# Output products of four branches in a two-layer trunk: one fp32 product, or three fp32r passes over high and low parts

## The chip, the cores and the metric

One core of a Trainium2 chip runs the whole program. The metric is the device time of one execution in microseconds; the time before is the median of three runs, 2294.9 us (2294.73 to 2297.84).

## The reference

Two layers of a hybrid decoder trunk on 512 tokens of width 1024. Per layer:

```
h = rms_norm(x, mix_norm_g[l])
p_gdn, p_mla, p_rwkv, p_dsa, p_gate = _split(h @ w_in[l], SLAB_SPLITS)
y_a = gdn_mixer(p_gdn, ...) @ w_out_gdn[l]
y_b = mla_mixer(p_mla, ...) @ w_out_mla[l]
y_c = rwkv7_mixer(p_rwkv, ...) @ w_out_rwkv[l]
y_d = dsa_mixer(p_dsa, ...) @ w_out_dsa[l]
g_a, g_b, g_c, g_d = _split(sigmoid(p_gate), GATE_SPLITS)
merged = g_a * y_a + g_b * y_b + g_c * y_c + g_d * y_d
x = x + merged @ w_o[l]
hm = rms_norm(x, mlp_norm_g[l])
x = x + square(relu(hm @ w_up[l])) @ w_down[l]
```

Each mixer's output is 512 tokens by 256 features, each `w_out_*` is 256 by 1024, each gate matrix 1024 by 1024. All is float32.

## The kernel before

Everything is held feature-major: a tile is 128 features by 512 tokens. Weights come as a stream of 134 units per layer (`unit_list`, L56), each a block of 1024 by 128 (8 tiles of 128x128), in the order of use. SyncE loads unit g into `ring[g % 3]` (L393). The large products are made in three passes over high and low parts, both of type fp32r: ScalarE copies the unit, rounded, to `w_hi[g % 2]` (`split_next`, L1046), GpSimd subtracts in two instructions of 128x512 to get `w_lo` (L425), and `split_product` (L458) multiplies `w_hi` by `h_hi` and `h_lo` (L464, L465, 16 matmuls), then waits for `split_lo` and multiplies `w_lo` by `h_hi` (L468, 8 matmuls). ScalarE calls `split_next` once for each unit whose product it has taken from its bank, and it has called it twice ahead of the first: after it has taken unit g it splits unit g + 2, so that two units at most are in split form. GpSimd follows it in the order of units.

The part of interest is the merge. Per branch there are eight "merge" units, the gate columns of 128 output features each, and with each comes an output block, 256 by 128 of that branch's `w_out`, which SyncE loads to `out_ring[n % 6]` (L398); n counts merge units over the whole program, 64 in all. TensorE makes the gates two at a time (`gates`, L500: two times 24 matmuls, into banks that ScalarE reads), and then the two outputs (`merge_outputs`, L518): each is two fp32 matmuls of 128x128 by 128x512 from `out_ring` and `yo` (L525). The branch output stands in `yo[:, slot]`, two buffers of 2x512 columns, written by VectorE (L1643 for RWKV, L1710 for DeltaNet, L1478 piece by piece in the two attentions). ScalarE takes a gate from its bank with a sigmoid into `sg[n % 2]` (`merge_sig`, L1009), before that waiting until output n - 2 has been merged (`mg_done`), and calls `split_next`. VectorE multiplies the output's bank by the gate and adds it to `mg` (`merge`, L1433), and signals `mg_done`.

Where the merges stand: RWKV (branch 2) has four outputs in one group (L784 to L788) and two pairs; DeltaNet (branch 0) four pairs, spread over the index scores of the sparse attention (L851 to L858); sparse attention (branch 3) a group of four after its own attention (L867 to L870) and two pairs; MLA (branch 1) a group of four (L917 to L920) and two pairs. In the groups of four of branches 3 and 1 the first two gates were made piecewise inside the attention (`gate_pieces`, L528). So a layer has 3 groups of four and 10 pairs. All engines run their queues strictly in the order of the code, each on its own, tied by semaphores.

GpSimd's queue holds, beside the subtractions, a few DMAs that wait: L435 (rotary tables) behind unit ("ds", 0), L438 behind unit ("merge", 3, 2).

Of the kernel before, what the change touches and what calls it, by code (L numbers as in the profile page):

```python
# [22 lines left out]
P = 128  # L23
# [134 lines left out]
def build(nc, x_in, pos_in, wstream, par_in, const_in, tabs, x_dram, out):  # L158
    ctx = ExitStack()
    with ctx:  # L160
# [11 lines left out]
        out_ring = sb("out_ring", [P, OUT_RING, 2, P])  # L172
# [4 lines left out]
        yo = sb("yo", [P, 2, 2, T])  # L177
# [74 lines left out]
        for name, n in (  # L252
# [20 lines left out]
            ("m_ss", 16), ("m_p", 16), ("m_pn", 16), ("m_pt", 16), ("m_o", 16),  # L273
            ("mg_sig", 32), ("mg_raw", 4), ("mg_done", 32), ("mg_hi", 8), ("mg_lo", 8), ("wo_done", 8), ("up_relu", 32), ("up_sq", 32), ("up_hi", 32), ("up_done", 32), ("g_zs", 1), ("r_s0", 1), ("g_s0", 1), ("down_done", 8 * QUARTERS),
# [49 lines left out]
        def merges_to(g):  # L324
# [32 lines left out]
            v=ar(25, (TT, 256)), tab=ar(27, (2, T)), ikz=ar(29, (2, T)), kz=ar(31, (2, 2, T)), tmp=ar(35, (T,)),  # L357
# [3 lines left out]
            tab=ar(17, (2, T)), tmp=ar(19, (T,)), bias=ar(20, (T,)), kr=ar(21, (T,)),  # L361
# [83 lines left out]
        def _(pe):  # L445
# [65 lines left out]
            def merge(l, br, slot, i, output=None):  # L511

                numbers = gates(l, br, i)
                if output:
                    pe.wait_ge(S[output], at(l, output, per[output]))
                merge_outputs(slot, numbers)
# [203 lines left out]
            for l in range(L):  # L720
# [65 lines left out]
                pe.wait_ge(S["r_out"], at(l, "r_out", 1))  # L786
                merge_outputs(0, numbers)
                merge_outputs(0, more)  # L788
# [15 lines left out]
                merge(l, 2, 0, 2)  # L804
                merge(l, 2, 0, 3)
# [36 lines left out]
                pe.wait_ge(S["d_vf"], at(l, "d_vf", 2))  # L842
                for half in range(2):
# [7 lines left out]
                for qt in range(1, TT):  # L851
                    if qt > 1:
                        index_scores(qt)
                    merge(l, 0, 1, qt - 1)
# [3 lines left out]
                merge(l, 0, 1, 3)  # L858
# [9 lines left out]
                pe.wait_ge(S["d_o"], at(l, "d_o", 16))  # L868
                merge_outputs(0, numbers)
                merge_outputs(0, more)  # L870
# [9 lines left out]
                merge(l, 3, 0, 2)  # L880
# [27 lines left out]
                merge(l, 3, 0, 3)  # L908
# [9 lines left out]
                pe.wait_ge(S["m_o"], at(l, "m_o", 16))  # L918
                merge_outputs(1, numbers)
                merge_outputs(1, more)  # L920
                for i in range(2, 4):
                    merge(l, 1, 1, i)
# [36 lines left out]
        def _(act):  # L959
# [48 lines left out]

            def merge_sig(l):  # L1009
                for _ in range(2):  # L1010
# [7 lines left out]
                    split_next()  # L1018

            def piecewise_sig(l, i):  # L1020

                if i in (GATE_STEPS[5], GATE_STEPS[11]):
# [5 lines left out]
                    split_next()  # L1028

# [54 lines left out]
            for l in range(L):  # L1084
# [88 lines left out]
                merge_sig(l)  # L1173
                merge_sig(l)
# [36 lines left out]
                for i in range(8):  # L1211
                    if i == 7:
# [29 lines left out]
                attention(l, "d", Dv, lambda i: piecewise_sig(l, i))  # L1242
                late_sig(l)
# [19 lines left out]
                attention(l, "m", Mv, lambda i: piecewise_sig(l, i))  # L1263
                late_sig(l)
# [43 lines left out]
        def _(dve):  # L1308
# [141 lines left out]
            def attention(l, x, V, scale, bias, slot, fill):  # L1450
# [517 lines left out]
```

## Time and profile before

| what | value |
|---|---|
| median of 3 runs | 2294.9 us |
| the profiled execution, its own time | 2294.88 us |
| its span | 2293.1 us |
| granted TensorE clock, mean over the span | 0.964 |
| TensorE matmuls busy | 2129.2 us, 93% |
| VectorE busy | 1241.2 us, 54% |
| ScalarE busy | 720.8 us, 31% |
| GpSimd busy | 740.5 us, 32% |

The profile is of one execution. The chain that ended last is followed back from the last instruction to the first, at each step to what released it. A row of the timeline merges instructions of one kind that follow each other on an engine; what stands in brackets is the engine's idle time before them and who ended it. fp32 matmuls appear as two instructions each. Ends of matmuls are modelled, with the next one's start ahead of them: the pace is read from starts.

### The profile page before, as it was taken

Reading aid. Unit: us, or ns where it says so; the run is one execution under the profiler, and the core shown is the slowest. Engines: PE = TensorE matmul, PEld = TensorE weight load, DVE = VectorE, ACT = ScalarE, POOL = GpSimd, SP = SyncE. Lnnn points to the kernel's source line nnn. Section 1 sums busy time; section 2 is a strip of 40 time slices with the busy share of each in tenths; the row PEclk is TensorE's granted clock in tenths of the full one; section 3 lists DMA queues with packets and bytes.
Section 4 is the critical chain, followed back from the end, with each engine's and each line's share of the span. In section 5 each row is a group of like instructions: output and inputs, shape, how many; then the busy total and the mean of one; then the engine's idle time right before and its main releaser. Section 6 shows DMA issues by size and latency. Waiting matters only on the chain.

```text
span 2293.1 us, 34619 instructions
## 1 busy us (share of the span) xinstructions
PE 2129.2 (93%) x14488; PEld 1654.4 (72%) x14488; DVE 1241.2 (54%) x1930; ACT 720.8 (31%) x1100; POOL 740.5 (32%) x550
## 2 busy tenths in 40 slices
PE   5988898998999999999989888899989999999997
PEld 3777677766666788888868766777656668888886
DVE  6785765798654332222358766568966544222223
ACT  3421321332333342323243133123242433423322
POOL 1530321332212444444434012123222144444442
PEclk7999998998999999999989999989999999999998
DMA  4320200221121232332232001012212122332321
GB/s 158 103 71 3 67 29 30 78 81 57 45 94 51 83 117 93 95 98 92 92 103 92 26 28 59 30 46 77 67 48 92 44 78 92 95 99 92 101 93 65
DMA packets 52266, 170.03 MB, mean 74 GB/s; under 512 B 5648, under 2 KB 13968, under 8 KB 51600
## 3 DMA queue, kind: packets, MB, share of 16 engines
q1 hardware_dynamic: 50928, 162.75, 22.2%
q0 software_dynamic: 1184, 5.07, 0.6%
q8 instruction: 116, 1.90, 0.3%
q14 instruction: 38, 0.31, 0.0%
HBM read 160.45 MB, written 7.34 MB: 73 GB/s over the span
## 4 chain that ended last, share of the span: by engine, by line
PE 76%; DVE 20%; ACT 2%; issue 2%; DMA 1%; SPq 0%; DVEq 0%; ACTq 0%
PE bank_a L464 11%; PE bank_a L465 11%; PE bank_a L468 11%; PE bank_v L468 7%; PE bank_v L464 7%; PE bank_v L465 6%; PE bank_v L583 5%; PE bank_v L525 3%; DVE arena L1752 2%; DVE m L1750 2%; DVE arena L1325 2%; PE bank_v L699 2%; DVE s_z L1425 1%; PE bank_v L681 1%; DVE mg L1331 1%
## 5 line engine op out<-in xcount | busy, mean ns | idle before, releaser
L425 POOL TENSOR_TENSOR w_lo<-ring,w_hi 128x512 fp32r<-128x512 f32 x536 | 734.1, 1392 | 1383.1 <-ACT w_hi L1046 1383.0
L464 PE MATMUL bank_a<-h_hi,w_hi 128*128 128x512 f32 x1440 | 587.3, 408 | 7.8 <-DVE h_lo L1359 4.8
L465 PE MATMUL bank_a<-h_lo,w_hi 128*128 128x512 f32 x1440 | 566.3, 393 | 0.0
L468 PE MATMUL bank_a<-h_hi,w_lo 128*128 128x512 f32 x1440 | 356.5, 390 | 0.0
L1046 ACT ACTIVATE w_hi<-ring 128x1024 fp32r<-128x1024 f32 x268 | 281.7, 1051 | 234.9 <-DVE arena L1867 220.5
L464 PEld LDWEIGHTS bank_a<-h_hi,w_hi 128*128 128x128 f32 x1440 | 272.9, 190 | 88.7 <-issue 18.8
L465 PEld LDWEIGHTS bank_a<-h_lo,w_hi 128*128 128x128 f32 x1440 | 273.6, 190 | 63.9 <-issue 9.3
L468 PEld LDWEIGHTS bank_a<-h_hi,w_lo 128*128 128x128 f32 x1440 | 270.8, 188 | 57.1 <-POOL w_lo L425 0.6
L1325 DVE TENSOR_TENSOR sg<-bank_v,sg 128x512 f32<-128x512 f32 x112 | 77.5, 692 | 339.7 <-PE bank_v L468 256.9
L464 PE MATMUL bank_v<-parts,w_hi 128*128 128x512 f32 x640 | 254.4, 398 | 1.4 <-DVE parts L1838 1.4
L465 PE MATMUL bank_v<-parts,w_hi 128*128 128x512 f32 x640 | 253.4, 396 | 0.0
L1857 DVE TENSOR_TENSOR arena<-arena 128x512 f32<-128x512 f32 x64 | 44.3, 692 | 244.8 <-ACT arena L1289 244.7
L468 PE MATMUL bank_v<-parts,w_lo 128*128 128x512 f32 x640 | 162.2, 396 | 0.0
L464 PEld LDWEIGHTS bank_v<-parts,w_hi 128*128 128x128 f32 x640 | 120.3, 188 | 32.7 <-DVE parts L1838 4.1
L465 PEld LDWEIGHTS bank_v<-parts,w_hi 128*128 128x128 f32 x640 | 120.2, 188 | 29.5 <-issue 0.5
L468 PEld LDWEIGHTS bank_v<-parts,w_lo 128*128 128x128 f32 x640 | 120.2, 188 | 29.1
L583 PE MATMUL bank_v<-arena 64*64 64x64 f32 x3712 | 114.1, 221 | 4.2 <-DVE arena L1397 4.2
L583 PEld LDWEIGHTS bank_v<-arena 64*64 64x64 f32 x3712 | 113.2, 138 | 4.9 <-DVE arena L1397 4.7
L525 PE MATMUL bank_v<-yo,out_ring 128*128 128x512 f32 x256 | 114.0, 592 | 0.0
L1325 DVE TENSOR_TENSOR arena<-arena 128x512 f32<-128x512 f32 (+5 forms) x80 | 96.7, 1209 | 23.4 <-ACT arena L1102 20.8
L1289 ACT ACTIVATE arena<-bank_a 128x512 f32<-128x512 f32 x64 | 38.3, 598 | 205.3 <-PE bank_a L468 205.3
L1016 ACT ACTIVATE sg<-bank_a 128x512 f32<-128x512 f32 x56 | 33.4, 597 | 217.8 <-PE bank_a L468 108.4
(277 smaller groups left out, 2450.3 us busy)
## 6 DMA issues: line engine op xcount, KB each, us to landing
ring<-in_w SPq DMA_DIRECT2D x268, 512.0 KB, 3.5
out_ring<-in_w SPq DMA_DIRECT2D x64, 128.0 KB, 3.5
x_dram<-arena SPq DMA_DIRECT2D x2, 2048.0 KB, 7.6
arena<-x_dram SPq DMA_DIRECT2D x2, 2048.0 KB, 7.9
arena<-in_x SPq DMA_DIRECT2D x2, 1024.0 KB, 8.7
arena<-tabs POOLq DMA_DIRECT2D x4, 512.0 KB, 3.9
out_x<-arena SPq DMA_DIRECT2D x2, 1024.0 KB, 4.3
par<-in_par POOLq DMA_DIRECT2D x2, 937.0 KB, 7.2
```

Source lines behind the costliest of these rows:

```text
L425: ins = nc.gpsimd.tensor_tensor(w_lo[:, g % SPLIT, ks, :], raw, w_hi[:, g % SPLIT, ks, :].bitcast(F32), ALU.subtract)
L464: mm(b[:], w_hi[:, s, k, :], hi[:, k, :], start=k == 0, stop=False)
L465: mm(b[:], w_hi[:, s, k, :], lo[:, k, :], start=False, stop=False)
L468: ins = mm(b[:], w_lo[:, s, k, :], hi[:, k, :], start=False, stop=k == KT - 1)
L525: ins = mm(b[:], out_ring[:, n % OUT_RING, k, :], yo[:, slot, k, :], start=k == 0, stop=k == 1)
L583: ins = mm(b[quarter(p_), k * C:(k + 1) * C], lhs[quarter(p_), m, :], rhs(m, p_), start=True, stop=True)
L699: ins = mm(b[rows, 0:P], v[:, k, h * C:(h + 1) * C], V_pt(x)[:, j % 2, k, :], start=k == 0, stop=k == qt)
L1046: act_fn(w_hi[:, g % SPLIT, :, :], ring[:, g % RING, :, :], ACT.Copy).then_inc(S["split_hi"], 1)
L1325: link(v.tensor_tensor(out_, a, b, op))
L1750: link(v.max(m8[:], src))
L1752: link(v.match_replace(wk, m8[:], src, -3e38))
L1857: v.tensor_tensor(relu2[:, n % 2, :], relu[:, n % 2, :], relu[:, n % 2, :], MUL).then_inc(S["up_sq"], 1)
```

## The change

The 64 outputs are made from high and low parts in three fp32r passes. ScalarE makes `out_hi` (one copy of 128x256 for each output block, `split_out`, right behind `split_next` of the same gate), GpSimd makes `out_lo` in place over `out_ring`. It does so for the output block of unit g - 2 behind its subtraction of unit g. TensorE waits for `ow_lo` at each output and makes six matmuls in place of two. The branch output stands in the arena, and ScalarE copies it to `y_hi` (2 x 128x512), VectorE subtracts to `y_lo` (2 x 128x512), once per branch and layer; there is one pair of such buffers, so that `y_hi` of a branch waits until the branch before is merged. The DMA of the rotary tables moves behind unit ("ds", 1).

```
-        out_ring = sb("out_ring", [P, OUT_RING, 2, P])
+        out_hi = sb("out_hi", [P, OUT_RING, 2, P], F32R)
+        with nc.sbuf_tensor("out_ring", [P, OUT_RING, 2, P], F32) as out_ring:
+            pass
+        out_lo = sb("out_lo", [P, OUT_RING, 2, P], F32R)
-        yo = sb("yo", [P, 2, 2, T])
+        y_hi = sb("y_hi", [P, 2, T], F32R)
+        y_lo = sb("y_lo", [P, 2, T], F32R)
...
                 ins.then_inc(S["split_lo"], 1)
+                if g >= SPLIT and UNITS[(g - SPLIT) % NU][0] == "merge":
+                    n = merges_to(g - SPLIT)
+                    pool.wait_ge(S["ow_hi"], n + 1)
+                    slot = n % OUT_RING
+                    nc.gpsimd.tensor_tensor(out_lo[:, slot, :, :], out_ring[:, slot, :, :], out_hi[:, slot, :, :].bitcast(F32), ALU.subtract).then_inc(S["ow_lo"], 1)
...
-                if UNITS[u] == ("ds", 0):
+                if UNITS[u] == ("ds", 1):
...
-            def merge_outputs(slot, numbers):
-                for j in range(2):
+            def merge_outputs(numbers):
+                for n in numbers:
                     b, reader, emptied = banks.next("v", "mg_done")
                     pe.wait_ge(reader, emptied)
-                    n = numbers[j]
-                    pe.wait_ge(out_here[n % OUT_RING], 16 * (n // OUT_RING + 1))
+                    pe.wait_ge(S["ow_lo"], n + 1)
+                    hi, lo = out_hi[:, n % OUT_RING], out_lo[:, n % OUT_RING]
                     for k in range(2):
-                        ins = mm(b[:], out_ring[:, n % OUT_RING, k, :], yo[:, slot, k, :], start=k == 0, stop=k == 1)
+                        mm(b[:], hi[:, k, :], y_hi[:, k, :], start=k == 0, stop=False)
+                        mm(b[:], hi[:, k, :], y_lo[:, k, :], start=False, stop=False)
+                    for k in range(2):
+                        ins = mm(b[:], lo[:, k, :], y_hi[:, k, :], start=False, stop=k == 1)
                     ins.then_inc(v_full, 1)
...
+            def split_out(n):
+
+                slot = n % OUT_RING
+                act.wait_ge(out_here[slot], 16 * (n // OUT_RING + 1))
+                act_fn(out_hi[:, slot, :, :], out_ring[:, slot, :, :], ACT.Copy).then_inc(S["ow_hi"], 1)
+
+            def high_output(l, src, need, k, branch):
+
+                act.wait_ge(S[need], at(l, need, k))
+                act.wait_ge(S["mg_done"], at(l, "mg_done", 8 * branch))
+                for f in range(2):
+                    act_fn(y_hi[:, f, :], src[:, f, :], ACT.Copy).then_inc(S["y_hi"], 1)
...
                     act_fn(sg[:, n % 2, :], b[:], ACT.Sigmoid).then_inc(S["mg_sig"], 1)
                     sigs[0] += 1
                     split_next()
+                    split_out(n)
...
+            def low_output(l, src, branch):
+
+                for f in range(2):
+                    dve.wait_ge(S["y_hi"], at(l, "y_hi", 2 * branch + f + 1))
+                    v.tensor_tensor(y_lo[:, f, :], src[:, f, :], y_hi[:, f, :].bitcast(F32), SUB).then_inc(S["y_lo"], 1)
```

`high_output` and `low_output` stand: for RWKV behind the first two gates of the group of four (ScalarE) and behind the last product of its output (VectorE); for DeltaNet at the fifth "ds" unit; for the two attentions at their ends. `piecewise_sig` calls `split_out` as `merge_sig` does. TensorE waits for `y_lo` where it waited for the branch output. SyncE's queue is as before.

How the queues move, at two places. First GpSimd around the last merge units of branch 2 (`w_lo` is a weight unit's low part, `out_lo` an output block's). Before:

```order
L425 TENSOR_TENSOR w_lo<-ring,w_hi 128x512 [waits split_hi]
L425 TENSOR_TENSOR w_lo<-ring,w_hi 128x512
L435 DMA arena<-tabs 128x2x512 [waits r_u,tab_out]
L425 TENSOR_TENSOR w_lo<-ring,w_hi 128x512 [waits split_hi]
L425 TENSOR_TENSOR w_lo<-ring,w_hi 128x512
```

And of the change, the same place with one unit more:

```order
L430 TENSOR_TENSOR w_lo<-ring,w_hi 128x512 [waits split_hi]
L430 TENSOR_TENSOR w_lo<-ring,w_hi 128x512
L436 TENSOR_TENSOR out_lo<-out_ring,out_hi 128x256 [waits ow_hi]
L430 TENSOR_TENSOR w_lo<-ring,w_hi 128x512 [waits split_hi]
L430 TENSOR_TENSOR w_lo<-ring,w_hi 128x512
L436 TENSOR_TENSOR out_lo<-out_ring,out_hi 128x256 [waits ow_hi]
L445 DMA arena<-tabs 128x2x512 [waits r_u,tab_out]
L430 TENSOR_TENSOR w_lo<-ring,w_hi 128x512 [waits split_hi]
```

Each subtraction of an output block stands behind both subtractions of the weight unit that is two further on.

Second TensorE at the last pair of branch 2 (`bank_a` takes a gate, `bank_v` an output; the second wait of an output is for its bank's last reader). Before:

```order
L468 MATMUL bank_a0<-h_hi,w_lo 128x512 [waits split_lo]
L468 MATMUL bank_a0<-h_hi,w_lo 128x512 x7
L525 MATMUL bank_v1<-yo,out_ring 128x512 [waits out_here0,g_row]
L525 MATMUL bank_v1<-yo,out_ring 128x512
L525 MATMUL bank_v2<-yo,out_ring 128x512 [waits out_here1,g_row]
L525 MATMUL bank_v2<-yo,out_ring 128x512
L558 MATMUL bank_a1<-consts,arena 128x128 [waits mg_sig,g_prep]
```

Of the change:

```order
L478 MATMUL bank_a0<-h_hi,w_lo 128x512 x7
L532 MATMUL bank_v1<-y_hi,out_hi 128x512 [waits ow_lo,g_row]
L533 MATMUL bank_v1<-y_lo,out_hi 128x512
L532 MATMUL bank_v1<-y_hi,out_hi 128x512
L533 MATMUL bank_v1<-y_lo,out_hi 128x512
L535 MATMUL bank_v1<-y_hi,out_lo 128x512 x2
L532 MATMUL bank_v2<-y_hi,out_hi 128x512 [waits ow_lo,g_row]
L533 MATMUL bank_v2<-y_lo,out_hi 128x512
L532 MATMUL bank_v2<-y_hi,out_hi 128x512
L533 MATMUL bank_v2<-y_lo,out_hi 128x512
L535 MATMUL bank_v2<-y_hi,out_lo 128x512 x2
L568 MATMUL bank_a1<-consts,arena 128x128 [waits mg_sig,g_prep]
```

The outputs' wait for a DMA has become a wait for GpSimd; nothing stands between the last gate and the two outputs, as before.

## Rows read from the trace of the kernel before

**Rows 1.** The page, the chain that ended last, shares of the span by engine.
```profile
PE 76%; DVE 20%; ACT 2%; issue 2%; DMA 1%; SPq 0%; DVEq 0%; ACTq 0%
```

**Rows 2.** The page, costliest groups: count, busy us, mean ns, idle before and releaser.
```profile
L525 PE MATMUL bank_v<-yo,out_ring 128*128 128x512 f32 x256 | 114.0, 592 | 0.0
```

**Rows 3.** Timeline, all engines, 597 to 613 us: start us, us, engine, line, operation.
```profile
597.87 1.98 PE L468 MATMUL bank_a<-h_hi,w_lo 128*128 128x512 f32 x8
...
603.31 1.98 PE L468 MATMUL bank_a<-h_hi,w_lo 128*128 128x512 f32 x8
605.12 7.03 PE L525 MATMUL bank_v<-yo,out_ring 128*128 128x512 f32 x16
...
608.61 0.60 ACT L1016 ACTIVATE sg<-bank_a 128x512 f32<-128x512 f32 x1 [13.17 <-DVE mg L1446]
...
610.23 2.95 POOL L425 TENSOR_TENSOR w_lo<-ring,w_hi 128x512 fp32r<-128x512 f32 x2 [12.07 <-ACT w_hi L1046]
```

**Rows 4.** Timeline, all engines, a pair of branch 0, 525 to 529 us.
```profile
525.15 3.59 PE L525 MATMUL bank_v<-yo,out_ring 128*128 128x512 f32 x8
525.35 0.60 ACT L1016 ACTIVATE sg<-bank_a 128x512 f32<-128x512 f32 x1 [3.89 <-PE bank_a L468]
525.84 1.05 ACT L1046 ACTIVATE w_hi<-ring 128x1024 fp32r<-128x1024 f32 x1
526.97 2.52 POOL L425 TENSOR_TENSOR w_lo<-ring,w_hi 128x512 fp32r<-128x512 f32 x2 [2.89 <-ACT w_hi L1046]
```

**Rows 5.** Groups by line and form, ScalarE: a form of 128x256.
```profile
L1209 ACT ACTIVATE arena<-bank_a 128x256 f32<-128x256 f32 x16 | 5.9, 383 | 5.3 <-DVE arena L1743 2.7 <-DVE arena L1740 2.0
```

**Rows 6.** Timeline, all engines, the group of four of branch 2, 267 to 278 us.
```profile
267.57 0.60 ACT L1016 ACTIVATE sg<-bank_a 128x512 f32<-128x512 f32 x1 [11.89 <-DVE mg L1442]
...
271.93 0.69 DVE L1442 TENSOR_TENSOR mg<-bank_v,sg 128x512 f32<-128x512 f32 x1 [1.02 <-PE bank_v L525]
...
278.02 7.87 PE L797 MATMUL bank_a<-consts,arena 128*128 128x128 f32 x48 [6.18 <-DVE arena L1660]
```

**Rows 7.** Timeline, all engines, a pair of branch 2, 299 to 310 us.
```profile
299.00 3.59 PE L525 MATMUL bank_v<-yo,out_ring 128*128 128x512 f32 x8
...
301.46 7.93 DVE L1325 TENSOR_TENSOR arena<-arena 128x1024 f32<-128x1024 f32 x4
301.56 8.98 POOL L425 TENSOR_TENSOR w_lo<-ring,w_hi 128x512 fp32r<-128x512 f32 x4 [27.44 <-ACT w_hi L1046]
```

**Rows 8.** Busy time by engine in windows, among the index scores: PE, PEld, DVE, ACT, POOL, PEclk.
```profile
434.00:552.00 118.00, 109.37 (x418) 77.40 (x416) 110.26 (x219) 36.20 (x56) 36.05 (x27) 0.97 0.22 69
```

**Rows 9.** Timeline, VectorE and ScalarE, first and last pair of branch 0.
```profile
474.88 0.69 DVE L1325 TENSOR_TENSOR sg<-bank_v,sg 128x512 f32<-128x512 f32 x1
...
546.90 0.60 ACT L1016 ACTIVATE sg<-bank_a 128x512 f32<-128x512 f32 x1 [20.01 <-DVE mg L1446]
...
551.10 0.92 DVE L1446 TENSOR_TENSOR mg<-mg,sg 128x512 f32<-128x512 f32 x1
```

**Rows 10.** Timeline, all engines, later pairs and the last group of four.
```profile
625.47 3.59 PE L525 MATMUL bank_v<-yo,out_ring 128*128 128x512 f32 x8
...
626.14 5.85 POOL L425 TENSOR_TENSOR w_lo<-ring,w_hi 128x512 fp32r<-128x512 f32 x4 [10.02 <-ACT w_hi L1046]
...
714.55 7.03 PE L525 MATMUL bank_v<-yo,out_ring 128*128 128x512 f32 x16
...
719.69 0.63 ACT L1272 ACTIVATE parts<-mg 128x512 fp32r<-128x512 f32 x1 [1.09 <-DVE mg L1446]
...
749.00 2.98 POOL L425 TENSOR_TENSOR w_lo<-ring,w_hi 128x512 fp32r<-128x512 f32 x2 [2.90 <-ACT w_hi L1046]
```

**Rows 11.** Timeline, TensorE, an idle wait in an attention.
```profile
663.99 0.30 PE L689 MATMUL bank_a<-consts,arena 128*128 128x128 f32 x1 [1.97 <-DVE arena L1471]
```

**Rows 12.** Windows behind waits of TensorE; columns as in rows 8.
```profile
665.10:668.40 3.30, 3.30 (x11) 2.27 (x10) 1.12 (x5) 0.66 (x3) 0.00 (x0) 0.50 0.01 3
...
276.00:282.70 6.70, 4.68 (x22) 4.68 (x23) 2.96 (x5) 2.50 (x4) 0.00 (x0) 0.50 0.11 45
```

More of the change, by code:

```diff
@@ L509, in gates, with merge @@
                 return numbers
[L511 to L516, printed above, removed]
-            def merge_outputs(slot, numbers):
-                for j in range(2):
+            def merge(l, br, i):
+                merge_outputs(gates(l, br, i))
+            def merge_outputs(numbers):
+                for n in numbers:
                     b, reader, emptied = banks.next("v", "mg_done")
                     pe.wait_ge(reader, emptied)
-                    n = numbers[j]
-                    pe.wait_ge(out_here[n % OUT_RING], 16 * (n // OUT_RING + 1))
+                    pe.wait_ge(S["ow_lo"], n + 1)
+                    hi, lo = out_hi[:, n % OUT_RING], out_lo[:, n % OUT_RING]
                     for k in range(2):
-                        ins = mm(b[:], out_ring[:, n % OUT_RING, k, :], yo[:, slot, k, :], start=k == 0, stop=k == 1)
+                        mm(b[:], hi[:, k, :], y_hi[:, k, :], start=k == 0, stop=False)
+                        mm(b[:], hi[:, k, :], y_lo[:, k, :], start=False, stop=False)
+                    for k in range(2):
+                        ins = mm(b[:], lo[:, k, :], y_hi[:, k, :], start=False, stop=k == 1)
                     ins.then_inc(v_full, 1)
@@ L785, in _ @@
                 more = gates(l, 2, 1)
-                pe.wait_ge(S["r_out"], at(l, "r_out", 1))
-                merge_outputs(0, numbers)
-                merge_outputs(0, more)
+                pe.wait_ge(S["y_lo"], at(l, "y_lo", 2))
+                merge_outputs(numbers)
+                merge_outputs(more)
                 pe.wait_ge(S["g_g"], at(l, "g_g", 2))
@@ L803, in _ @@
                     chunk_products("v", "g_row", half, G["g_of"], lambda m, p_: cst("upto")[quarter(p_), quarter(p_)])
-                merge(l, 2, 0, 2)
-                merge(l, 2, 0, 3)
+                merge(l, 2, 2)
+                merge(l, 2, 3)
                 pe.wait_ge(S["g_prep"], at(l, "g_prep", 1))
@@ L853, in _ @@
                         index_scores(qt)
-                    merge(l, 0, 1, qt - 1)
+                    merge(l, 0, qt - 1)
                     if qt == 2:
@@ L857, in _ @@
                             feat_group(("cq", i), l, h_hi, h_lo, "a", "m_in")
-                merge(l, 0, 1, 3)
+                merge(l, 0, 3)
                 numbers = []
@@ L867, in _ @@
                 more = gates(l, 3, 1)
-                pe.wait_ge(S["d_o"], at(l, "d_o", 16))
-                merge_outputs(0, numbers)
-                merge_outputs(0, more)
+                pe.wait_ge(S["y_lo"], at(l, "y_lo", 6))
+                merge_outputs(numbers)
+                merge_outputs(more)
                 pe.wait_ge(S["m_sq"], at(l, "m_sq", 1))
@@ L879, in _ @@
                 mm(b[:], cst("ones"), Mv["sq"][:, 2, :], start=True, stop=True).then_inc(v_full, 1)
-                merge(l, 3, 0, 2)
+                merge(l, 3, 2)
                 pe.wait_ge(S["m_c"], at(l, "m_c", 1))
@@ L917, in _ @@
                 more = gates(l, 1, 1)
-                pe.wait_ge(S["m_o"], at(l, "m_o", 16))
-                merge_outputs(1, numbers)
-                merge_outputs(1, more)
+                pe.wait_ge(S["y_lo"], at(l, "y_lo", 8))
+                merge_outputs(numbers)
+                merge_outputs(more)
                 for i in range(2, 4):
-                    merge(l, 1, 1, i)
+                    merge(l, 1, i)
                 for i in range(8):
```

32 lines of the change are left out of this document (22 added, 10 removed).

## Prediction, made before the changed kernel was run

> **What bounds the kernel now.** I read the chain that ended last first: TensorE holds 76% of the span and VectorE 20% [rows 1]. So what lengthens TensorE's own queue counts nearly everywhere, and what it must wait for counts too. The groups give the size of what is changed: the output products are 256 instructions and 114.0 us busy [rows 2]. GpSimd looks free in the shares, but each of its steps follows a ScalarE step, which follows a gate; the timeline around a merge shows this chain [rows 4], and there the change is decided.
>
> **What the new products save.** Two low passes of 8 matmuls in successive gates start 5.44 us apart, with 24 fp32r matmuls between [rows 3]: 0.227 us each. The group of four outputs takes 7.03 us for 16 fp32 instructions, the last of them 0.59 long, so (7.03 - 0.59) / 15 = 0.429 each [rows 2, 3]. An output falls from 4 x 0.429 = 1.72 us to 6 x 0.227 = 1.36 us. For 64 outputs that is 23 us, all of it on TensorE. This is the whole gain.
>
> **What the split costs by itself.** ScalarE's new copy of an output block has 256 columns. The nearest row of that width takes 0.38 us, a conversion of 512 columns 0.63 [rows 5, 10]: I take 0.42. GpSimd's new subtraction has 256 columns. Two of 512 take 2.52 us undisturbed [rows 4], so one takes 1.26; half of it is 0.63, the whole is the upper end, and I take 0.75, near the half. The copies and subtractions of the branch outputs (2 x 0.63 on ScalarE, 2 x 0.7 on VectorE, eight times) fall where both wait: ScalarE idles 11.89 us before the third sigmoid of a group and 20.01 before a late pair [rows 6, 9]. If that cover were gone they would cost 8 x 2 = 16 us; I take 3 us for all of this with the two extra copies in each attention.
>
> **The new wait.** The order of GpSimd's queue puts the low part of output n behind both subtractions of the weight unit two further on, and that unit is split by ScalarE only after it has taken gate n. For the first output of a pair this has happened a gate (5.44 us) earlier. For the second it has not even begun when TensorE arrives. Take the undisturbed pair [rows 4]. The outputs begin at 525.15, ScalarE takes the second gate at 525.35 and splits until 526.89, GpSimd works from 526.97 to 529.49. Only then comes the new subtraction, to 530.25, and TensorE can begin the second output at 530.3 and end it at 531.7. Now it is through at 525.15 + 8 x 0.429 = 528.6. So a pair loses 3.1 us, its own saving of 0.7 already counted. Behind TensorE's wait stand the next two gates, whose weights are long ready, so nothing fills it.
>
> Per layer there are ten pairs and three groups of four; the times of layer 0 follow.
>
> - Group of branch 2. The third sigmoid starts at 267.57 [rows 6], because it waits for the first output's merge. Split to 269.2, GpSimd to 271.8, new subtraction to 272.6, third output; then GpSimd's next unit to 275.1, 275.9, fourth output to 277.3, merged at 278.2 in place of 272.6 [rows 6]. TensorE's work at 278.02 waited for VectorE by then, so it moves too: +5.6.
> - Next pair. GpSimd needs 8.98 us for four subtractions here while VectorE works on two SBUF operands [rows 7]: 2.25 each, 1.8 times the quiet one. First half to 306.1, new subtraction (1.2) to 307.3, second half to 311.8, then 0.75 and 1.36: 314.0 instead of 299.00 + 3.44 = 302.4. +11.6.
> - Last pair of branch 2, quiet: +3.1.
> - The four pairs of branch 0 stand in a stretch where VectorE is busy 110.26 of 118 us and TensorE has slack [rows 8]. The first pair is taken at once by VectorE (its second output at 474.88 [rows 9]): +3.5. The next two are consumed tens of us later: 0. In the last one, ScalarE waits for VectorE until 546.90 [rows 9]; by the same steps, with TensorE at half its rate as it is there, the fourth merge ends at 559.3 instead of 552.0: +7.
> - Group of branch 3 [rows 3]. The third sigmoid moves from 608.61 to 608.25, split to 609.8, GpSimd 2.95 to 612.8, 613.6; its next unit to 616.4, 617.1; output to 618.5. Now 605.12 + 6.87 = 612.0: +6.5.
> - Its pairs. In the first, four subtractions run in one piece of 5.85 from 626.14 [rows 10]; with two new ones between, the second output ends at 635.0 against 625.47 + 3.44 = 628.9: +6.1. The second, with 2.98 for two subtractions as in a later pair [rows 10]: +3.6.
> - Group of branch 1: two copies of 0.63 into the merge's high part stand ahead of the third sigmoid [rows 10], so the sigmoid comes at 719.9, and the end at 730.0 against 714.55 + 6.87 = 721.4 [rows 10]: +8.6. Its pairs, with 2.98: +3.6 each, 7.2.
>
> Sum per layer: 5.6 + 11.6 + 3.1 + 3.5 + 7 + 6.5 + 6.1 + 3.6 + 8.6 + 7.2 = 62.8 us; the second layer repeats it: 126 us.
>
> **The clock.** TensorE now idles 4 to 8 us at each of these places. After an idle wait of 1.97 us in an attention [rows 11] it ran at 0.50 of full speed (1.2 GHz) from 665.1 to 668.4, with no idle time in it [rows 12]: 1.7 us lost. After 6.2 us of idle time the clock was 0.50 from 276.0 to 282.7 [rows 6, 12]. Outside branch 0 and the first group, where TensorE waits anyway, eight places per layer get such a wait on the path: 16 x 1.7 = 27 us if each is punished; bounds 0 and, at twice the price, 54. I take 22.
>
> A rule speaks of GpSimd's price beside VectorE. The row shows 2.25 us for what takes 1.26 alone [rows 7]. The Trainium skill, "SBUF — State Buffer", section "SBUF: two separate sides", says that the two share a port pair that is locked for a whole instruction, so that the loser blocks entirely. By it the new subtraction would be late by a whole VectorE instruction and not by a factor: 0.75 + 1.0 instead of 1.2 at the pair of branch 2, and likewise in the six places where 2.95 or more was needed for two; the sum would be some 12 us more. No row has a GpSimd instruction this short, so the trace does not decide it.
>
> Sum: the profiled execution, 2294.88 (span 2293.1), which is the median 2294.9 within 0.1 us; + 126 + 22 + 3 = **2446 us**, 6.6% slower. This kernel's measurement can tell about 0.2% (5 us) from no change.
>
> **Rivals.**
> - The wait is absorbed: part of it lies where TensorE or ScalarE later waits for VectorE, and the clock does not fall. For it: VectorE carries 20% of the chain. Against it: most places are followed by gates that run back to back. Half of the 126 and no clock loss: 2294.9 + 63 + 3 = 2361; two thirds, 2382.
> - Faster: TensorE never waits for `ow_lo`. Then only the products count: 2294.9 - 23 + 3 = 2275. The place is the second output of each pair; it decides if the low part is there 1.36 us after the outputs begin, at 526.5 in the pair of rows 4. Against it: GpSimd starts the subtraction ahead of it only at 526.97. It would need the queue order to be other than listed, or a change that does not do what it says.
> - Worse: the low clock persists between waits that lie 11 us apart, and the new subtraction costs nearly a full one. 54 for the clock, and 0.5 us for each of some 32 subtractions on the path, 16: 2295 + 126 + 54 + 16 + 3 = 2494.
>
> **The numbers.** Forecast: 0.72, of which a quarter for the port rule's 2458. Absorbed: 0.15. Worse: 0.10. Faster: 0.02, no change 0.01. The forecast's own bounds are 2420 (no clock loss, 0.63 us for each of the 32 subtractions on the path) and 2478 (54 us of clock loss). The range goes some 20 us further down, into the absorbed case, and a few up into the worse one: 2398 to 2482, which leaves out about 2 in 10. Faster by over 0.2%: 0.02; within: 0.01; slower: 0.97.
>
> **What would show it.** In the changed profile: an output of six matmuls in 1.36 us; TensorE idle ahead of the second output's first matmul (L532), 3 to 4 us in a pair, ended by GpSimd's L436, in all some 130 us; each L436 between 0.6 and 1.3 us long; GpSimd's share of the chain up from nothing to several per cent; a granted clock under the 0.964 of before; the MLP stretch unchanged. I am wrong if L532's idle time is below 60 us, if L436 comes before the unit's subtractions, or if the idle time is there and VectorE's waits shrink by as much.

## Result: 6.1% slower, and the profile after

The changed kernel takes 2435.8 us (median of four runs, 2429.0 to 2438.9); the kernel before took 2295.4 beside it (2294.7 to 2297.8). The ratio is 1.0608, with a 95% interval of 1.0585 to 1.0632. The profiled execution took 2438.2 us, with a span of 2436.4 and a mean granted clock of 0.939; before it was 2293.1 and 0.964. So the span grew by 143.3 us. The forecast was 2446.

The page of the changed kernel: the busy line, then the first line of the chain that ended last, to be set against [rows 1].

```profile
PE 2157.6 (89%) x14616; PEld 1706.3 (70%) x14616; DVE 1254.0 (51%) x1946; ACT 749.5 (31%) x1180; POOL 780.2 (32%) x614
...
PE 74%; DVE 15%; POOL 5%; ACT 3%; issue 2%; DMA 1%; SPq 0%; DVEq 0%; ACTq 0%
```

GpSimd stood in no part of the chain before and now holds 5% of it, though its busy share is 32% as before. This is a wait and not a load. TensorE, whose work was to shrink, is busy 28 us more, because many of its matmuls took longer each (the means below).

Groups by line; after the bar busy us, mean ns, idle before and its releaser. The first three answer to [rows 2].

```profile
L532 PE MATMUL bank_v<-y_hi,out_hi 128*128 128x512 f32 x128 | 67.3, 525 | 137.4 <-POOL out_lo L436 137.4
L533 PE MATMUL bank_v<-y_lo,out_hi 128*128 128x512 f32 x128 | 63.0, 492 | 0.0
L535 PE MATMUL bank_v<-y_hi,out_lo 128*128 128x512 f32 x128 | 52.9, 504 | 0.0
L436 POOL TENSOR_TENSOR out_lo<-out_ring,out_hi 128x256 fp32r<-128x256 f32 x64 | 54.4, 850 | 0.0
L1024 ACT ACTIVATE out_hi<-out_ring 128x256 fp32r<-128x256 f32 x64 | 26.1, 408 | 0.0
L1485 DVE TENSOR_TENSOR y_lo<-arena,y_hi 128x512 fp32r<-128x512 f32 x16 | 18.5, 1194 | 4.7 <-ACT y_hi L1031 4.6
```

One number explains most of the result: TensorE sat idle for 137.4 us ahead of L532, each time until GpSimd's L436. The means of 492 to 525 ns, against the 390 of a matmul at full clock, say that many of these products ran at the low clock (0.63 us each in the stretch at 1.2 GHz shown below).

The third pair of branch 0, the one that the prediction took as its model [rows 4], in the timeline of the changed kernel (start us, us, engine, line; in brackets the idle time before and who ended it).

```profile
560.14 0.40 PE L532 MATMUL bank_v<-y_hi,out_hi 128*128 128x512 f32 x1
...
560.34 0.60 ACT L1040 ACTIVATE sg<-bank_a 128x512 f32<-128x512 f32 x1 [3.59 <-PE bank_a L478]
...
560.83 1.05 ACT L1072 ACTIVATE w_hi<-ring 128x1024 fp32r<-128x1024 f32 x1
...
561.78 0.41 ACT L1024 ACTIVATE out_hi<-out_ring 128x256 fp32r<-128x256 f32 x1
561.96 2.49 POOL L430 TENSOR_TENSOR w_lo<-ring,w_hi 128x512 fp32r<-128x512 f32 x2 [2.19 <-ACT w_hi L1072]
...
564.41 0.73 POOL L436 TENSOR_TENSOR out_lo<-out_ring,out_hi 128x256 fp32r<-128x256 f32 x1
...
565.28 0.47 PE L532 MATMUL bank_v<-y_hi,out_hi 128*128 128x512 f32 x1 [3.58 <-POOL out_lo L436]
...
567.41 0.63 PE L474 MATMUL bank_a<-h_hi,w_hi 128*128 128x512 f32 x1
```

Read it from the sigmoid down. ScalarE takes the second gate at 560.34 and splits unit g + 2; GpSimd begins at 561.96 and needs 2.49 us for that unit, which TensorE does not want yet; only then come the 0.73 us that TensorE waits for. The second output starts 5.14 us after the first and not 1.39. The gates then resume at 567.41, 7.27 after the pair's start, where they took 3.03 before.

The clock behind this wait: busy time in a window (PE, PEld, DVE, ACT, POOL, then PEclk), as in [rows 12].

```profile
566.20:569.30 3.10, 3.10 (x9) 2.42 (x8) 2.96 (x8) 0.00 (x0) 0.00 (x0) 0.50 0.32 128
```

TensorE had been idle 3.58 us, had nothing to wait for from 565.28 on, and ran at 1.2 GHz from 566.2 to 569.3, so some 1.5 us are lost here.

The first pair behind the group of branch 2 answers to [rows 7].

```profile
308.00 7.30 DVE L1356 TENSOR_TENSOR arena<-arena 128x1024 f32<-128x1024 f32 x4
308.10 4.45 POOL L430 TENSOR_TENSOR w_lo<-ring,w_hi 128x512 fp32r<-128x512 f32 x2 [31.78 <-ACT w_hi L1072]
...
312.51 1.70 POOL L436 TENSOR_TENSOR out_lo<-out_ring,out_hi 128x256 fp32r<-128x256 f32 x1
...
314.18 4.46 POOL L430 TENSOR_TENSOR w_lo<-ring,w_hi 128x512 fp32r<-128x512 f32 x2
...
314.36 0.77 PE L532 MATMUL bank_v<-y_hi,out_hi 128*128 128x512 f32 x1 [8.65 <-POOL out_lo L436]
```

Here even the first output waits, 8.65 us. ScalarE comes late: it takes the pair's first gate only at 306.48, 0.8 us after TensorE has reached the outputs, so GpSimd begins only at 308.10. And GpSimd is slower beside VectorE, while both work on SBUF operands: its pair of subtractions takes 4.45 us in place of 2.49, and the new one 1.70 in place of 0.73.

### The profile page after: what moved, and what is told of

It reads as the page before. It is cut to its first block, busy times and chain, and to the rows that moved or that the text cites. A ratio compares the mean times of both kernels' runs of the same rounds, so it can differ in the third digit from the quotient of the medians.

```text
span 2436.4 us, 35047 instructions
## 1 busy us (share of the span) xinstructions
PE 2157.6 (89%) x14616; PEld 1706.3 (70%) x14616; DVE 1254.0 (51%) x1946; ACT 749.5 (31%) x1180; POOL 780.2 (32%) x614
## 4 chain that ended last, share of the span: by engine, by line
PE 74%; DVE 15%; POOL 5%; ACT 3%; issue 2%; DMA 1%; SPq 0%; DVEq 0%; ACTq 0%
PE bank_a L474 11%; PE bank_a L475 11%; PE bank_a L478 11%; PE bank_v L474 6%; PE bank_v L475 6%; PE bank_v L478 6%; PE bank_v L593 5%; POOL w_lo L430 4%; PE bank_v L709 2%; DVE s_z L1456 1%; ACT w_hi L1072 1%; POOL out_lo L436 1%; DVE arena L1356 1%; PE bank_v L691 1%; DVE mg L1362 1%
## 5 line engine op out<-in xcount | busy, mean ns | idle before, releaser
L430 POOL TENSOR_TENSOR w_lo<-ring,w_hi 128x512 fp32r<-128x512 f32 x536 | 722.5, 1369 | 1483.8 <-ACT w_hi L1072 1483.7
L532 PE MATMUL bank_v<-y_hi,out_hi 128*128 128x512 f32 x128 | 67.3, 525 | 137.4 <-POOL out_lo L436 137.4
L532 PEld LDWEIGHTS bank_v<-y_hi,out_hi 128*128 128x128 f32 x128 | 29.8, 233 | 162.7 <-issue 155.8
```

The costliest lines, as they stand in the source:

```text
L430: ins = nc.gpsimd.tensor_tensor(w_lo[:, g % SPLIT, ks, :], raw, w_hi[:, g % SPLIT, ks, :].bitcast(F32), ALU.subtract)
L532: mm(b[:], hi[:, k, :], y_hi[:, k, :], start=k == 0, stop=False)
```

## Experiments

Two questions were open. Is the loss the place of the split in GpSimd's and ScalarE's queues, and not the three passes? And why does the saving on TensorE not show? A first set of four kernels took the order, the passes and the clock apart (e1 to e4); of a second set, e5 to e7 priced the passes and the parts of the split work in the better order and e8 the clock once more; the last two split only half of the outputs. The expectation of each was written before it ran. The comparison kernel is always the kernel before, run on the same chip.

### e1_early: the output block is split with its own gate unit

```
-                if g >= SPLIT and UNITS[(g - SPLIT) % NU][0] == "merge":
-                    n = merges_to(g - SPLIT)
+                if UNITS[u][0] == "merge":
+                    n = merges_to(g)
```
```
     # at the end of split_next, in place of the two calls behind it
+                    if UNITS[g % NU][0] == "merge":
+                        split_out(merges_to(g))
```

> Every output block is split together with its own gate unit (ScalarE and GpSimd, two units ahead of the gate's product) and not two units later. Same work, same instructions, other order. Theory A (the loss is TensorE's wait for the late low part, and the clock that falls with it): the waits vanish, what is left is the saving of the products, 2295 - 23 + 3 to 8 for the splits = 2275 to 2290. Theory B (the loss is the added work on ScalarE, GpSimd and VectorE, and their contention): the order matters little, above 2380.

Measured: 2299.3 us, ratio 1.0016 (1.0008 to 1.0025). All 64 outputs are still split and made in three passes; only the place of two instructions in two queues differs, and 136.5 of the 140.4 us are gone. TensorE is not idle once ahead of L532 now. Its longest waits are others (waited for, us in total, times, longest):

```profile
PE bank_v L648 <- DVE s_z L1456: 29.1, 28, 1.3
PE bank_a L699 <- DVE arena L1508: 14.2, 9, 2.8
```

So the queue order is the cause of the loss. But the expected 2275 to 2290 was missed by 9 us: without that wait the kernel should have been 20 us faster than before and it is 4 slower. e5 to e7 follow that up.

### e2_pool_first: only GpSimd's order changed

The block with `out_lo` is moved ahead of the wait for `split_hi` of the next unit and of that unit's two subtractions. ScalarE still makes `out_hi` only behind the gate.

```
+                if g >= SPLIT and UNITS[(g - SPLIT) % NU][0] == "merge":
+                    ...
+                    nc.gpsimd.tensor_tensor(out_lo[:, slot, :, :], ...)
                 pool.wait_ge(S["split_hi"], g + 1)
```

> Only GpSimd's order changes: the subtraction of an output block goes ahead of the two subtractions of the weight unit two further on, ScalarE's order stays. Theory A: the second output of a pair waits for sigmoid, split, copy and one short subtraction, about 1.7 us in place of 3.6, and the pair loses 1.0 in place of 3.1; groups of four lose some 2.5 us less each. Per layer about 33 us of loss in place of 63, and less of the clock: 2360 to 2390. Theory B: as the change, 2425 to 2440.

Measured: 2362.8 us, ratio 1.0296 (1.0282 to 1.0310), inside Theory A's range. The third pair of branch 0 now waits 1.44 us and not 3.58. What stays is ScalarE's half of the chain, sigmoid, 1.05 us of `w_hi`, 0.41 of `out_hi`, then 0.72 on GpSimd:

```profile
PE bank_v L532 <- POOL out_lo L430: 85.8, 38, 9.0
```

The GpSimd order is worth 73 us and, once that is changed, the ScalarE order the other 63.5.

### e3_one_pass: two of the six products

TensorE makes only the products of high parts; the low parts are made and waited for, but unused. Two of the three passes are left out of the computation.

```
-                        mm(b[:], hi[:, k, :], y_hi[:, k, :], start=k == 0, stop=False)
-                        mm(b[:], hi[:, k, :], y_lo[:, k, :], start=False, stop=False)
-                    for k in range(2):
-                        ins = mm(b[:], lo[:, k, :], y_hi[:, k, :], start=False, stop=k == 1)
+                        ins = mm(b[:], hi[:, k, :], y_hi[:, k, :], start=k == 0, stop=k == 1)
```

> The change with one pass only (high weights by high outputs): two fp32r matmuls per output in place of six, 4 x 0.227 = 0.91 us less per output, 58 us less of TensorE's work in all. The low parts are still made and waited for, but not used. Theory A: in a pair the first output's saving only lengthens the wait for the second, so a pair gains 0.91 and a group of four 0.9 to 1.8; 26 places give 24 to 35 us: 2400 to 2412. If the products' own time were on the path throughout: 2436 - 58 = 2378.

Measured: 2419.8 us, ratio 1.0540 (1.0524 to 1.0556), 8 us above Theory A's range. Of the products' 64 x 0.91 = 58 us, which TensorE no longer executes, only 16 reach the end. The group says where the rest is:

```profile
L532 PE MATMUL bank_v<-y_hi,out_hi 128*128 128x512 f32 x128 | 59.8, 567 | 180.2 <-POOL out_lo L436 180.2
```

The wait grows from 137.4 to 180.2 us. These 43 us more of waiting are what is missing from the 58: a faster first output only arrives sooner at the same GpSimd instruction. In the changed kernel the three passes set little of the time.

### e4_fill and e8_fill_waits: products in the wait, for the clock

Four fp32 products that nobody uses, eight instructions of 0.429 us or 3.4 us in all, are put ahead of the second output. (The expectation of e8 gives 1.72 us for them, which is half of it; that of e4 has it right.) e4 does it in all 20 pairs:

```
+                    if pair and n == numbers[1]:
+                        for _ in range(4):
+                            mm(b[:], cst("ones"), consts[:, 0:T], start=True, stop=True)
```

> The change with eight instructions of unused fp32 products (four matmuls of 512 columns, 3.4 us) ahead of the second output of each of the 20 pairs, into its own bank before it is started: TensorE is busy where it waited 3.6 to 4 us. Theory C (each wait is punished by a stretch at 1.2 GHz, 1.7 us lost, on 12 to 16 of the pairs): the granted clock rises from 0.939 to 0.95 or more and the time falls by 10 to 25 us, to 2411 to 2426. If the clock costs nothing: 2436 or a few us above.

Measured: 2434.3 us, ratio 1.0604 (1.0589 to 1.0618), no more than 1.6 us under the changed kernel: the expected time was missed, although the granted clock rose as expected, to 0.952 or 0.953 from the 0.938 to 0.943 of the changed kernel. Compared place by place, the pairs with a full wait became shorter (first pair of branch 1, 7.00 us from the first output to the next gate, where it had been 7.91), but the first pair of branch 3 went from 4.64 to 9.02, since its second output had only 0.26 us to wait and the 3.4 us of the fill came on top. So the run did not isolate the clock, and e8 fills only the 14 pairs whose second output waits 3.3 to 4 us:

```
-                merge_outputs(gates(l, br, i))
+                merge_outputs(gates(l, br, i), (br, i) not in ((2, 2), (3, 2), (0, 3)))
```

> Edit, on the changed kernel (2435.8 us): four unused fp32 products (1.72 us) ahead of the second output of those 14 pairs alone whose second output waits 3.3 to 4 us for GpSimd; the other places stay as they are. In the run with all 20 pairs filled these 14 became about 1 us shorter each and the others 11 us longer in sum. Theory A, the low clock behind a wait of 3.6 us costs some 1 us and the fill avoids it: 2417 to 2427 us. Theory B, the fill takes nothing from the time (no clock cost): 2433 to 2438 us.

Measured: 2419.1 us, ratio 1.0535 (1.0521 to 1.0550), inside Theory A's range: 16.7 us, or 1.2 per pair. The two ratios with their intervals leave 10 to 23 us, or 0.7 to 1.6 per pair. The granted clock rises from 0.938 to 0.943 in the changed kernel to 0.947 to 0.952 here. Adding unused work to TensorE makes the kernel faster. The same pair as above, with the filled wait:

```profile
557.38 0.63 PE L538 MATMUL bank_v<-y_hi,out_lo 128*128 128x512 f32 x2
557.85 3.59 PE L531 MATMUL bank_v<-consts 128*128 128x512 f32 x8
561.51 0.50 PE L535 MATMUL bank_v<-y_hi,out_hi 128*128 128x512 f32 x1
```

The fill runs through the wait, and the second output begins 5.06 us after the pair's start at 556.45, where it had been 5.14: the length of the wait is GpSimd's, the fill changes only what follows. The 12 places that are not filled keep what they had, so the clock's share is 16.7 us or more.

### e5_fp32_early: the old products in the new order

On e1, with all splits made and waited for, each output is again two fp32 matmuls, of the high parts. The low parts' share of the output is left out.

```
-                        mm(b[:], hi[:, k, :], y_hi[:, k, :], start=k == 0, stop=False)
...
+                        ins = mm(b[:], hi[:, k, :].bitcast(F32), y_hi[:, k, :].bitcast(F32), start=k == 0, stop=k == 1)
```

> Edit, on the kernel with the early split of e1 (2299.3 us): the splits are all made and waited for as there, but TensorE makes each output as two fp32 matmuls of the high parts (four instructions, 1.72 us, as in the kernel before) in place of six fp32r matmuls (1.36 us); the output then lacks the low parts' share. Theory A, the products' 0.36 us x 64 = 23 us are saved in e1 and the work of splitting costs some 27 us: 64 x 0.36 more than e1, less the 8 outputs per layer of branch 0 where TensorE has slack (6 us), so 2316 us (2312 to 2323). Theory B, most of the saving never reached the end in e1 (other engines set the pace by then) and the splitting costs little: 2299 to 2307 us.

Measured: 2304.8 us, ratio 1.0035 (1.0022 to 1.0048). This is Theory B. The three passes save 5.5 us at the end (4.4 by the two ratios, whose intervals leave 1 to 8), not 23; the splitting by itself costs 9.1 against the kernel before beside it, 2295.7 (5 to 11 by the interval). In the trace the saving exists and is lost again. TensorE in e1 leads e5 by 0.64 us more after each pair, and by 4.6 us behind branch 2's last pair in layer 1; at branch 0's third pair, some 210 us later, the two are level. Two things take the lead away there. Windows of e1, then of e5:

```profile
1493.40:1517.30 23.90, 18.14 (x165) 15.39 (x166) 10.07 (x31) 1.66 (x6) 0.00 (x0) 0.50 0.00 1
434.00:552.00 118.00, 107.27 (x434) 80.05 (x432) 109.43 (x216) 34.61 (x59) 40.48 (x33) 0.98 0.22 69
```
```profile
1503.40:1517.00 13.60, 10.04 (x102) 8.63 (x103) 5.78 (x20) 1.11 (x4) 0.00 (x0) 0.50 0.01 2
434.00:552.00 118.00, 110.31 (x427) 78.19 (x425) 110.40 (x216) 34.60 (x59) 43.53 (x34) 1.00 0.22 69
```

In the DeltaNet scan of layer 1, where TensorE waits for VectorE again and again, the clock was at 1.2 GHz for 23.9 us in e1 and for 13.6 in e5 (2.8 us of the lead, by the starts of the same instructions). And in branch 0's stretch VectorE is busy 109 to 110 of 118 us in both, as it was before [rows 8]: it sets the pace there, and TensorE's shorter products become idle time.

The clock needs care. In layer 0 the same scan is the other way round, 20.5 us at 1.2 GHz in e1 and 23.9 in e5, so that scan alone shows nothing regular. But over the whole kernel the clock is lower in e1 in every run: the mean over a run lay between 0.954 and 0.961 in e1, e6 and e7, the three kernels that make six fp32r matmuls for each output in this order, and between 0.962 and 0.964 in e5 with its fp32 products; the kernel before had 0.961 to 0.967. A mean lower by 0.007 is 16 us of TensorE's work at most, and less where TensorE waits anyway. So the clock goes with the products and not with the subtractions (e6 lacks GpSimd's, e7 VectorE's), and it can hold a good part of the missing saving; how much, and why it falls, was not tried apart.

### e6_no_low_block and e7_no_low_branch: the price of the splitting

Both on e1, with the count of matmuls kept. e6 leaves out GpSimd's `out_lo` (TensorE takes `out_hi` in the third pass too), e7 leaves out VectorE's `y_lo` (TensorE takes `y_hi` in the second pass too); each output lacks that part.

```
-                    pe.wait_ge(S["ow_lo"], n + 1)
-                    hi, lo = out_hi[:, n % OUT_RING], out_lo[:, n % OUT_RING]
+                    pe.wait_ge(S["ow_hi"], n + 1)
+                    hi, lo = out_hi[:, n % OUT_RING], out_hi[:, n % OUT_RING]
```
```
-                low_output(l, R["o"], 0)
...
-                        mm(b[:], hi[:, k, :], y_lo[:, k, :], start=False, stop=False)
+                        mm(b[:], hi[:, k, :], y_hi[:, k, :], start=False, stop=False)
```

> Edit, on e1: GpSimd makes no low part of the output block; TensorE waits for the high part and uses it in the third pass too (same count of matmuls; the output is changed). It prices GpSimd's 64 subtractions. Theory A, beside VectorE they hold up both engines (the port pair) and the weight units behind them, in the stretch ahead of branch 2's group and in branch 0's: e1 less 8 to 14 us, 2285 to 2291 us. Theory B, GpSimd has room and they cost nothing: 2297 to 2301 us.

> Edit, on e1: VectorE makes no low part of the branch outputs (16 subtractions of 128x512 left out), TensorE waits for the high part and uses it in the second pass too (same count of matmuls; the output is changed). It prices VectorE's 16 subtractions, 1.3 us each beside GpSimd at branch 2, 0.7 elsewhere. Theory A, they lie on the path at all four branches: e1 less 8 x 1.4 = 11 us and more, 2284 to 2289 us. Theory B, they lie beside TensorE's gates except in branch 0's stretch: e1 less 0 to 4 us, 2295 to 2300 us.

Measured: e6 2289.5 us, ratio 0.9968 (0.9956 to 0.9981), so GpSimd's 64 subtractions cost 9.8 us (11.0 by the two ratios), Theory A; e7 2297.0 us, ratio 1.0007 (0.9998 to 1.0016), so VectorE's 16 cost 2.3 at the most likely, Theory B, though this interval and that of e1 overlap and it may be nothing. TensorE does not wait for a single one of GpSimd's 64, and yet they cost 0.15 us each. One such place is in the timelines ahead of branch 2's group, e1 first (L1661 is a VectorE instruction that multiplies 128x2048 elements, called the product here):

```profile
237.15 3.24 DVE L1661 TENSOR_TENSOR arena<-arena 128x2048 f32<-128x2048 f32 x1
...
233.26 1.71 POOL L436 TENSOR_TENSOR out_lo<-out_ring,out_hi 128x256 fp32r<-128x256 f32 x1
236.97 4.55 POOL L430 TENSOR_TENSOR w_lo<-ring,w_hi 128x512 fp32r<-128x512 f32 x2 [2.00 <-ACT w_hi L1070]
...
240.45 5.40 PE L681 MATMUL bank_v<-arena,consts 128*128 128x512 f32 x8 [3.42 <-DVE arena L1661]
```

And the kernel before, where the same product is L1624:

```profile
237.15 2.29 DVE L1624 TENSOR_TENSOR arena<-arena 128x2048 f32<-128x2048 f32 x1
...
237.38 4.41 POOL L425 TENSOR_TENSOR w_lo<-ring,w_hi 128x512 fp32r<-128x512 f32 x2 [3.68 <-ACT w_hi L1046]
```

The product takes 2.29 us where it begins 0.23 ahead of GpSimd, and 3.24 where GpSimd began 0.18 ahead of it. It pays the rest of GpSimd's first instruction, about 1 us, and TensorE waits for it. The product begins behind GpSimd in e1 because VectorE's two instructions ahead of it take 4.94 us in place of 4.53, with L436 beside the second. In e6, where L436 is gone, the same product begins 0.24 us ahead of GpSimd and takes 2.29 us again. This is one place in each layer; that all of the 9.8 us arise in this way was not shown, but e1 falls behind e6 on TensorE between the merges and not in them: at 23 of the 26 places by 0.01 us or less.

### e9_half_early and e10_half_late: only the outputs of branches 3 and 1

If the cost lies in branches 2 and 0, where VectorE is busy, and the gain in 3 and 1, half of the change should be better than all of it. Both kernels keep fp32 products for branches 2 and 0, e9 in the order of e1, e10 in that of the changed kernel. Everything is computed.

```
+        def is_split(n):
+            return n % 32 >= 16
...
+                    if not is_split(n):
+                        pe.wait_ge(out_here[n % OUT_RING], 16 * (n // OUT_RING + 1))
+                        for k in range(2):
+                            ins = mm(b[:], out_ring[:, n % OUT_RING, k, :], yo[:, n % 32 // 8, k, :], start=k == 0, stop=k == 1)
```

> Edit, on e1 (early split, 2299.3 us): only the outputs of branches 3 and 1 (32 of 64) are split and made in three passes; branches 2 and 0 keep their fp32 products, their output written straight into its buffer as in the kernel before. Everything is computed. From the traces of e1 against before: TensorE was 5.3 us late at the end of branch 0's stretch and 1.6 us late at the end of the layer, so the second half of a layer gained 3.7 us, in layer 1 5.4 us. Theory A, the loss of e1 lies in branches 2 and 0 and the gain in 3 and 1: before less 9, so 2286 us (2284 to 2289). Theory B, what layer 0 gains is given back where VectorE sets the pace in layer 1 (the lead of e1 over e5 was gone there): before less 5, 2290 us (2289 to 2292). Theory C, no gain: 2293 to 2297 us.

> Edit, on the changed kernel (order of the splits as it has it, 2435.8 us): only the outputs of branches 3 and 1 are split and made in three passes; branches 2 and 0 keep their fp32 products. Everything is computed. Theory A, the waits add up place by place: from branch 3's group to the end of the layer the changed kernel fell behind by 34.4 us in layer 0 and 34.4 in layer 1, so before plus 69: 2364 us (2360 to 2369). By the prediction's own terms it is 32 x 2 = 64 and 10 places' share of the clock, 14: 2373 us. Theory B, the delays of the two halves of a layer are not independent (a late first half makes the waits of the second longer, or hides them): under 2355 or over 2375 us.

Measured: e9 2292.7 us, ratio 0.9987 (0.9978 to 0.9996), e10 2363.6 us, ratio 1.0296 (1.0282 to 1.0310). e10 hits Theory A: the waits add up place by place, and a layer's late half does not depend on its early one. e9 is the only version that computes everything and is under the kernel before, by 2.8 us or 0.13%: its interval just leaves 1 out, and it is less than the 0.2% that the prediction asks for. It lies between Theory B and C. In its profiled execution branches 3 and 1 gained 6.0 us in layer 0 and 2.6 in layer 1, as Theory A has it; but that one took 2287.5 us, the lower end of its twelve (2287.5 to 2296.2), with the highest granted clock of them, 0.965. The four slowest, 2294.7 to 2296.2 us, had 0.958 to 0.961. So the median gains less at a lower clock; why the clock varies from run to run is open.

## Why the prediction was right

**The products.** Predicted 1.36 us for an output in place of 1.72. Start to start it is 1.39 (643.82 to 645.21 in branch 3's group, 531.15 to 532.54 in e1), and the pairs of e1 are 0.64 shorter, not 0.72. The step "For 64 outputs that is 23 us, all of it on TensorE", called there the whole gain, is the one that was wrong in kind: on TensorE, yes, but 5.5 us at the end (e1 against e5), since VectorE sets the pace around branch 0 and the clock is lower. In the forecast this did no harm, because the places were worked out one by one there and two of branch 0's four pairs were put at 0. In the rival "faster", 2275, it did: with all waits gone the kernel takes 2299.

**The split instructions.** ScalarE's copy 0.42 predicted, 0.41 measured. GpSimd's 0.75 predicted; the median of the 64 is 0.73, but the mean 0.85, since those beside VectorE take up to 1.70. The "3 us for all of this", the rest of the splitting, was too small, if 9.1 us in e5's comparison is its price. Most of that seems to be GpSimd's hold on VectorE (9.8 us in e6), which the prediction had put into the pairs alone.

**The new wait.** The model pair: predicted to start its second output 5.15 us after the first, measured 5.14. TensorE's idle time ahead of L532 was to be "some 130 us"; it is 137.4. Place by place in layer 0, predicted and then measured (how much later TensorE's next work comes than before, less what it was late already):

| place | predicted | measured |
|---|---|---|
| group of branch 2 | 5.6 | 6.4 |
| next pair | 11.6 | 13.7 |
| last pair of branch 2 | 3.1 | 4.5 |
| branch 0, to its end | 10.5 | 14.1 |
| group of branch 3 | 6.5 | 7.1 |
| its two pairs | 9.7 | 10.2 |
| group of branch 1, with the attention before | 8.6 | 6.7 |
| its two pairs | 7.2 | 10.3 |
| layer 0 | 62.8 | 73.0 |

Layer 1 measured 70.9. The measured column holds the clock's loss, the predicted one doesn't; the surplus of 10.2 us in the layer is near what the prediction had put down to the clock, 11 for each layer, though not all of it is the clock's. Where no other cause is in sight it has that size: 3.1 us for the two pairs of branch 1. Two places had more: the next pair, whose 1.70 us for the new subtraction is 0.5 over the 1.2 taken, and the stretch ahead of branch 0's first pair, 1.8 us, in which the scan stands for which no term was set.

Inside branch 0 the sum fits by luck. The terms were 3.5, 0, 0 and 7. VectorE, which sets the pace there, fell behind by 5.1 us at the first pair, 3.6 at the second, 0 at the third, and at the fourth by 6.3, of which it had won back 3.0 before branch 3. So of the two pairs put at nothing one was not absorbed, and the last cost half of its term. The model pair, the third, cost TensorE 4.2 us and VectorE nothing, as its 0 had it.

**The clock.** Predicted 22 us with bounds of 0 and 54. The reading behind it has a slip: in [rows 12] the low clock begins at 276.0, 2 us before the wait that ends at 278.02 [rows 6] is over, so not all of its 6.7 us are work lost. The 14 filled pairs give 16.7, that is 1.2 us for each where the prediction took 1.7 [rows 12], though for fewer places, 16 against 14 here and 12 more that were not filled. At the same price those would make 14, and some of them stand where TensorE waits anyway. So 17 to 31 us, and 22 lies among them, with a price too high and a count too low. Where it falls was not as predicted either, and that the total fits is partly luck: over the terms of their places, branches 3 and 1, with six of the layer's eight places that had a clock price, measured 2.3 us more in layer 0, and branches 2 and 0, with the other two, 7.9 more. e10 says the same of the late half: 78 us by the prediction's terms, 68 measured.

**The sum.** 143.9 us late at the end of layer 1 and 143.3 at the end of the span: the MLP stretches neither lost nor gained, as forecast. Against 126 + 22 + 3 = 151 the forecast is 8 us high: 4 of them stand at the end of layer 1 (148 against 143.9), where layer 1 was 2.2 us cheaper than layer 0 and the prediction had repeated it, and 3 are the term for the other splits, which the measured places hold already.

**The port.** The prediction set 1.2 us (a factor of 1.8, from [rows 7]) against 0.75 + 1.0 for the new subtraction at the pair of branch 2. It took 1.70 there and in the same place of layer 1, 1.71 at 233 us in e1. So a short instruction is not slowed by a factor: the new one takes 0.97 us more than its quiet 0.73, and each of the two longer ones ahead of it 0.98 more than its quiet 1.25. It also lies outside the 0.6 to 1.3 us that the prediction named for L436. The Trainium skill, "SBUF — State Buffer", section "SBUF: two separate sides", says that VectorE and GpSimd share a port pair which one of them locks for a whole instruction; these rows agree with that rule, and L1661's extra 0.95 us shows the same hold from VectorE's side. The 12 us more that it was to add to the sum did not appear, since few places had VectorE instructions of this kind beside them: 16 of the 64 took over 0.9 us.

**The rivals.** Absorbed (2361): 137.4 us of wait stand beside 143.3 us of time. VectorE's share of the chain did fall, from 20% to 15%, but a share tells of one path; of the places only the last three pairs of branch 0 and the attention ahead of branch 1's group let some of their wait go. Worse (2494): the clock came back between waits. Faster: L436 came behind the unit's subtractions, as listed.

## What to carry to other kernels

When an operand gets one more preparation step on another engine, look for where that step stands in that engine's queue before counting what it saves: here two instructions of 0.4 and 0.7 us, placed behind work for two units further on, cost 136 us more than in their own unit's place, where the whole change costs 4. A saving on an engine, even one that is busy 93% of the span, is not a saving of time in the stretches where another engine sets the pace; add it up by stretch, with the chain of waits at hand. And count a helper on GpSimd also by what it does to VectorE's two-operand instructions beside it, not only by whether anybody waits for it.

## What the runs showed of the hardware

- A wait of 3.3 to 4 us costs TensorE some 1.2 us more behind it at 1.2 GHz (16.7 us for 14 pairs, e8, with 10 to 23 left by the intervals), and four unused products in the wait avoid it. This was expected in kind; that a kernel gets 0.7% faster by it was not.
- GpSimd's subtraction of 128x256 takes 0.73 us and up to 1.70 beside VectorE's two-operand instructions, and one of 128x512 takes 2.25 in place of 1.25: nearly the same time is added to both (0.97 and 0.98 us at 308 to 314 us). A VectorE product of 2.29 us took 3.24 when GpSimd's instruction had begun 0.18 us before it. Which of the two begins first decides who waits.
- 64 GpSimd instructions for which nobody waits cost 9.8 us of 2299 (e6), 0.15 each.
- With six fp32r matmuls for each output in place of four fp32 instructions, the granted clock was 0.954 to 0.961 in every run of e1, e6 and e7, and 0.962 to 0.964 in e5. The cause was not tried.
